# Output projection of a two-layer decoder trunk in fp32r pieces, with its weights split during the attention

## The reference, cut to what matters

```python
def nsa_mixer(h, w_in, w_out, ...):
    q, kc_raw, vc_raw, ks, vs, kw, vw, gates = jnp.split(h @ w_in, splits, axis=-1)
    ...
    o = g[:, :, 0] * heads(o_cmp) + g[:, :, 1] * heads(o_slc) + g[:, :, 2] * heads(o_win)
    return o.reshape(B, S, D_MODEL) @ w_out
def moba_mixer(h, w_in, w_out):
    q, k, v = jnp.split(h @ w_in, 3, axis=-1)
    ...
    return _merge_chunks(o) @ w_out
def reference(x, ...):
    for layer in range(DEPTH):
        mix = nsa_mixer(...) if layer % 2 == 0 else moba_mixer(...)
        x = layer_norm(DN_ALPHA * x + mix, ln_g[layer, 0], ln_b[layer, 0])
        ffn = grouped_moe(x, router_w, router_bias, moe_w_gate[layer], moe_w_up[layer], moe_w_down[layer])
        x = layer_norm(DN_ALPHA * x + ffn, ln_g[layer, 1], ln_b[layer, 1])
    return x
```

## Time and profile before

| what | us |
|---|---|
| median of 3 runs | 779.02 (777.27 to 779.57) |
| profiled execution, its own time | 778.95 |
| span in its profile | 777.2 |
| PE busy in the span | 740.8 (95%) |
| DVE busy | 285.3 (37%) |
| ACT busy | 184.4 (24%) |
| POOL busy | 95.2 (12%) |

### The profile page before, as it was taken

One profiled execution on the slowest core, in us unless ns is written; L12 is line 12 of the kernel. 1 busy time (PEld: TensorE's weight loads), 2 busy tenths in 40 slices (PEclk: granted clock), 3 DMA queues, 4 the chain that ended last, 5 costly groups with the idle time before them and its releaser, 6 DMA issues.

```text
span 777.2 us, 9026 instructions
## 1 busy us (share of the span) xinstructions
PE 740.8 (95%) x3721; PEld 392.2 (50%) x3721; DVE 285.3 (37%) x544; ACT 184.4 (24%) x424; POOL 95.2 (12%) x80
## 2 busy tenths in 40 slices
PE   6999999999999999999969999999999999999984
PEld 5877755556334443443337887645634344434331
DVE  4484676335112211221154774623522121212115
ACT  4443655133011101110131455613300110011100
POOL 0011244212000000000042220411200000000000
PEclk9999999999999999999988999999999999999997
DMA  9999600118899999999999955012799999999991
GB/s 281 367 385 423 280 1 2 55 66 307 341 409 432 428 427 428 428 428 420 421 390 387 387 199 198 20 55 108 280 401 400 429 428 428 429 428 426 421 412 63
DMA packets 41388, 245.05 MB, mean 315 GB/s; under 512 B 5760, under 2 KB 9984, under 8 KB 27008
## 3 DMA queue, kind: packets, MB, share of 16 engines
q1 hardware_dynamic: 41344, 244.43, 78.2%
HBM read 243.37 MB, written 1.05 MB: 315 GB/s over the span
## 4 chain that ended last, share of the span: by engine, by line
PE 80%; DMA 8%; DVE 8%; issue 2%; ACT 1%; SPq 0%; POOL 0%; DVEq 0%
PE ps L751 24%; PE ps L772 13%; DMA ring<-in_w_up 7%; PE ps L674 7%; PE ps L522 4%; PE ps L524 4%; PE ps L523 4%; PE ps L736 3%; PE ps L782 3%; PE ps L615 2%; PE ps L599 1%; PE ps L681 1%; PE ps L539 1%; PE ps L580 1%; PE ps L540 1%
## 5 line engine op out<-in xcount | busy, mean ns | idle before, releaser
L751 PE MATMUL ps<-ring,R 128*64 128x512 f32 x928 | 227.1, 595 | 0.0
L751 PEld LDWEIGHTS ps<-ring,R 128*64 128x64 f32 x928 | 70.5, 137 | 108.5 <-issue 106.9
L772 PE MATMUL ps<-ring,R 128*64 128x512 f32 x448 | 113.5, 596 | 0.0
L1001 ACT ACTIVATE wh<-ps,small 128x512 fp32r<-128x512 f32 x32 | 22.0, 688 | 264.7 <-PE ps L772 263.1
L1284 DVE TENSOR_TENSOR wl<-ring,wh 128x512 fp32r<-128x512 f32 x72 | 54.9, 778 | 46.6 <-ACT wh L979 46.3
L772 PEld LDWEIGHTS ps<-ring,R 128*64 128x64 f32 x448 | 35.2, 137 | 66.9 <-issue 63.8
L1478 DVE SCALAR_TENSOR_TENSOR wl<-ps,small,wh 128x512 fp32r<-128x512 f32 x32 | 24.0, 751 | 104.7 <-ACT wh L1001 104.0
L674 PE MATMUL ps<-ring,R 128*128 128x512 f32 x128 | 57.9, 598 | 0.9 <-DVE R L1591 0.9
L522 PE MATMUL ps<-wh,xh 128*128 128x512 f32 x144 | 57.9, 402 | 0.7 <-DVE wl L1284 0.6
L979 ACT CAST wh<-ring 128x512 fp32r<-128x512 f32 x72 | 44.4, 621 | 55.1 <-PE ps L524 51.5
L523 PE MATMUL ps<-wl,xh 128*128 128x512 f32 x144 | 56.9, 395 | 0.0
(11 more groups left out here) (177 smaller groups left out, 951.4 us busy)
## 6 DMA issues: line engine op xcount, KB each, us to landing
ring<-in_w_gate SPq DMA_DIRECT2D x28, 2048.0 KB, 16.9
ring<-in_w_up SPq DMA_DIRECT2D x22, 2048.0 KB, 18.0
ring<-in_w_down SPq DMA_DIRECT2D x22, 2048.0 KB, 19.6
ring<-in_w_in SPq DMA_DIRECT2D x22, 1024.0 KB, 14.2
ring<-in_w_down SPq DMA_DIRECT2D x12, 1024.0 KB, 26.5
ring<-in_w_out SPq DMA_DIRECT2D x8, 1024.0 KB, 14.7
R<-in_w_up SPq DMA_DIRECT2D x4, 2048.0 KB, 17.7
ring<-in_w_up SPq DMA_DIRECT2D x8, 1024.0 KB, 15.8
```

The costliest lines, as they stand in the source:

```text
L751: last = mm(ps[64 * e:64 * e + 64, to, :], xe[:, j, at + 64 * e:at + 64 * e + 64], slots[e][:, j * UNIT:(j + 1) * UNIT], start=(j == 0), s ...
L772: last = mm(ps[64 * e:64 * e + 64, 2 + w, :], hT[:, k, 64 * e:64 * e + 64], slots[e][:, at:at + UNIT], start=(k == 0), stop=(k == FJ - 1))
```

## The change

**Output projection.** In layer 0 pieces 0 to 6, in layer 1 pieces 0 to 4, of both halves, become three fp32r products each (`PIECED`); the others stay in float32. The high parts of these weights (`WO_HI`) are cast on ACT during the attention, behind the exponentials of an item, by the table `WO_AT` (so many pieces behind item m): one behind each item from 2 to 15 in layer 0 (14 pieces), and 1, 2, 1, 2, 1, 2, 1 behind items 1 to 7 in layer 1 (10 pieces). They go to `xh`, `xl`, `wh`, `wl`, which are free then. The rest of an item's first piece is subtracted on POOL behind the scaling of that item, over the weights in the slot; a second piece's rest is subtracted on DVE, one step later, behind the copy of the probabilities. The attention's own output is split on DVE as it leaves PSUM, a cast and a subtraction in place of one copy. PE waits for all rests of the layer before the first piece.

**Filling products.** `keep_warm` adds products of 128x512 whose result nobody reads: 9 ahead of the first transposes of layer 0 and 7 behind them, 14 and 5 in layer 1. At the start they work on tiles that DVE sets to zero (`blank`). The transposes of tile 1 stand behind piece 6 (layer 0) and piece 4 (layer 1) of tile 0.

**Layer norm behind the experts.** `ln_scale` writes to PSUM, over its own source, and `ln_shift` reads it there. The statistics of tile 1's first half stand behind tile 0's layer norm.

**Order.** SP loads the whole first unit ahead of the second tile of x, and loads the second norm's weights (and waits for the normalised rows) behind all of the layer's experts. ACT starts the first unit's casts one piece into the tokens' casts; it casts the first tile's rows behind `rows_copy(1, 0)` and `score(0)`. ACT and DVE load the count of full slots in the second pair of experts and not behind all of them. Y, the routing's copy of the rows, lies in R4 and no longer in R2.

The diff, cut to its core:

```diff
+        R5r, R6r = R56r[:, 0:3 * D], R56r[:, 3 * D:6 * D]
+        OT_HI = [R6r[:, 1536 + j * S:1536 + (j + 1) * S] for j in range(6)] + [R5r[:, 2560:2560 + S]]
+        OT_LO = [R2r[:, j * S:(j + 1) * S] for j in range(7)]
+        OT2_HI = [R6r[:, 1536 + u * 512:2048 + u * 512] for u in range(3)]
+        OT2_LO = [R2r[:, u * 512:(u + 1) * 512] for u in range(3)]
+        flat = [v[:, :, :].rearrange("p j t -> p (j t)").rearrange("p (n c) -> p n c", c=UNIT) for v in (xh, xl)]
+        WO_HI = [[flat[0][:, 0], flat[0][:, 1], flat[1][:, 0], flat[1][:, 1], wh[:, 0], flat[0][:, 2], flat[0][:, 3]],
+                 [flat[1][:, 2], flat[1][:, 3], wh[:, 1], wh[:, 2], wl[:, 0], wl[:, 1], wl[:, 2]]]
+        PIECED = [7, 5]
+        WO_AT = [[0] * 2 + [1] * 14, [0] + [1, 2] * 3 + [1]]
+        WO = [[(w, j) for w in range(2) for j in range(n)] for n in PIECED]
...
-        Y = R2[:, :].rearrange("p (a c) -> p a c", a=T)
+        Y = R4[:, :].rearrange("p (a c) -> p a c", a=T)
...
+        def wo_lo_at(l, w, j):
+            return slot_r[SLOT_OF[AT[("unit", OUT[2 * l + w])]]][:, j * UNIT:(j + 1) * UNIT]
...
+        def wo_chunks(l, m):
+            first, many = sum(WO_AT[l][:m]), WO_AT[l][m]
+            return [(first + n, WO[l][first + n]) for n in range(many)]
...
-            load_unit(0, 0, 1)
+            load_unit(0)
             sp.dma_start(X[:, 1], x[P:2 * P]).then_inc(x_in[1], 16)
-            load_unit(0, 1, 2)
...
-                sp.wait_ge(N.x_ready, ready(2 * l, T - 1, 1))
-                load_ln(2 * l + 1, R.ln_in)
                 load_halves(6 * PAIRS * l + SLOT + 1)
                 for n in range(SLOT + 3, LASTROUND):
                     load_expert(6 * PAIRS * l + n)
                 for n in range(LASTROUND, 6 * PAIRS, 2):
                     load_halves(6 * PAIRS * l + n)
+                sp.wait_ge(N.x_ready, ready(2 * l, T - 1, 1))
+                load_ln(2 * l + 1, R.ln_in)
...
+            def keep_warm(bank, n):
+                for _ in range(n):
+                    mm(ps[:, bank, :], identb[:, :], bc(causalb[:, :], 1, 4), start=True, stop=True, skip_group_check=True)
...
-                        if a == 0 and j == 3:
+                        if a == 0 and j == (6, 4)[l]:
...
+                if a == 0 and w == 0 and js.start == 0:
+                    pe.wait_ge(wo_lo, (14, 24)[l])
                 for j in js:
                     if a == 0 and w == 0:
                         pe.wait_ge(L.ot_sb, B.ot_sb + j + 1)
-                    if a == 0 and j % 4 == 0:
-                        pe.wait_ge(*landing(("unit", u), j // 4))
-                    last = mm(ps[:, 2 * a + w, :], OT[j][:, a * P:(a + 1) * P],
-                              in_slot(("unit", u))[:, j * UNIT:(j + 1) * UNIT],
-                              start=False, stop=(j == KJ - 1), skip_group_check=True)
+                    if a == 0 and j == PIECED[l]:
+                        pe.wait_ge(*landing(("unit", u), 1))
+                    to, tok = ps[:, 2 * a + w, :], slice(a * P, (a + 1) * P)
+                    if j >= PIECED[l]:
+                        last = mm(to, OT[j][:, tok], in_slot(("unit", u))[:, j * UNIT:(j + 1) * UNIT],
+                                  start=False, stop=(j == KJ - 1), skip_group_check=True)
+                    else:
+                        mm(to, OT_HI[j][:, tok], WO_HI[w][j], start=False, stop=False, skip_group_check=True)
+                        mm(to, OT_HI[j][:, tok], wo_lo_at(l, w, j), start=False, stop=False, skip_group_check=True)
+                        last = mm(to, OT_LO[j][:, tok], WO_HI[w][j], start=False, stop=False, skip_group_check=True)
...
+                keep_warm(4 if l == 0 else 1, (9, 14)[l])
+                if l == 0:
+                    pe.wait_ge(ident_in, 16)
                 transpose_x(l, 0)
+                keep_warm(4, (7, 5)[l])
...
-                    x_hi(0)
-                    first_unit_hi()
+                    x_hi(0, (0,))
+                    first_unit_hi(range(0, 1))
+                    x_hi(0, (1,))
+                    first_unit_hi(range(1, KJ))
...
+                    for n_, (w, j) in wo_chunks(l, m):
+                        act.wait_ge(*landing(("unit", OUT[2 * l + w]), j // 4))
+                        copy(WO_HI[w][j], in_slot(("unit", OUT[2 * l + w]))[:, j * UNIT:(j + 1) * UNIT]).then_inc(wo_hi, 1)
...
                 for i in range(PAIRS):
                     n, g = PAIRS * l + i, DUOS * l + i // 2
+                    if i == 1:
+                        act.wait_ge(R.over, rbase[l].over + 1)
+                        most = act.value_load(over[0:1, 0:1], min_val=0, max_val=S)
                     act.wait_ge(rd.gate_done, n + 1)
...
+                    if a == 0 and w == 0:
+                        act.wait_ge(L.mix, B.mix + 3)
...
+                rows_copy(1, 0)
+                score(0)
                 rows_hi(0, 0)
                 rows_hi(0, 1)
-                rows_copy(1, 0)
-                score(0)
...
+                    for n, (w, j) in wo_chunks(l, m):
+                        if n == wo_chunks(l, m)[0][0]:
+                            pool.wait_ge(wo_hi, len(WO[0]) * l + n + 1)
+                            tt(wo_lo_at(l, w, j), in_slot(("unit", OUT[2 * l + w]))[:, j * UNIT:(j + 1) * UNIT], WO_HI[w][j],
+                               ALU.subtract).then_inc(wo_lo, 1)
...
-                    ln_scale(t, w, bank).then_inc(dve_step, 1)
+                    ln_scale(t, w, bank, ps[:, bank + w, :] if k % 2 else None).then_inc(dve_step, 1)
...
-                    ln_shift(t, w).then_inc(N.x_ready, 1)
+                    ln_shift(t, w, ps[:, bank + w, :] if k % 2 else None).then_inc(N.x_ready, 1)
...
+                    split_x(0, 0, (0,))
...
+                    for c, (w, j) in wo_chunks(l, m - 1)[1:] if 1 <= m < n else []:
+                        dve.wait_ge(wo_hi, len(WO[0]) * l + c + 1)
+                        tt(wo_lo_at(l, w, j), in_slot(("unit", OUT[2 * l + w]))[:, j * UNIT:(j + 1) * UNIT], WO_HI[w][j],
+                           ALU.subtract).then_inc(wo_lo, 1)
                     if m >= 4 and m % T:
                         dve.wait_ge(L.pv, B.pv + m - 3)
                         u = (m - 4) // T
-                        if l == 0:
+                        if l == 0 and u < 7:
+                            step(copy(OT_HI[u], ps[:, 6 + u % 2, 0:S]))
+                            tt(OT_LO[u], ps[:, 6 + u % 2, 0:S], OT_HI[u], ALU.subtract).then_inc(L.ot_sb, 1)
+                        elif l == 0:
                             copy(OT[u], ps[:, 6 + u % 2, 0:S]).then_inc(L.ot_sb, 1)
+                        elif u < 2:
+                            step(copy(OT2_HI[u], ps[:, 6 + u % 2, :]))
+                            tt(OT2_LO[u], ps[:, 6 + u % 2, :], OT2_HI[u], ALU.subtract).then_inc(L.ot_sb, 2)
+                        elif u == 2:
+                            step(copy(OT_HI[4], ps[:, 6 + u % 2, 0:S]))
+                            tt(OT_LO[4], ps[:, 6 + u % 2, 0:S], OT_HI[4], ALU.subtract).then_inc(L.ot_sb, 1)
+                            copy(OT[5], ps[:, 6 + u % 2, S:2 * S]).then_inc(L.ot_sb, 1)
...
-                half_stats(1, 0, 6, main.comb, n + 2)
                 step(half_stats(0, 1, 4, main.comb, n + 3))
                 layer_norm(2 * l + 1, 0, 4, R.ln_in, C.ln_in + 32)
+                half_stats(1, 0, 6, main.comb, n + 2)
```

## The result

The changed kernel takes 773.35 us (median of 13 runs, 770.99 to 776.04) against 777.83 us before (median of 13 runs): the ratio is 0.9936, with a 95% interval of 0.9924 to 0.9948, so 4 to 6 us are won. The forecast was 769.6 us in a range of 764.5 to 775.0. The direction and the range hold; the size does not: about half of the 9.3 us arrived. The kernel before is 1.1 us faster here than the 778.95 us that the forecast started from, so the gap in the time, 3.8 us, looks smaller than the gap in the gain, 4.3 to 4.8 us.

The account below looks back on a forecast made before the run. The prediction took PE as the bound (80% of the span), plus attention's ring and the layer boundary. From 778.95 us, -7.8 + 0.3 + 2.9 - 1.8 - 2.9 = -9.3 gave 769.6 us, range 764.5 to 775.0.

Parts of the forecast that it names:

- The products: Output projections: fp32r pieces gain 0.16 us each, 7.8 us in all, 4.55 in layer 0 and 3.25 in layer 1.
- Rival (e): Output projections: fp32r pieces with both operands newly written are no cheaper; 777.4 us; chance 0.08, shared with Rival (c).
- The row splits moved behind the scores are read only behind the whole projection: Projection and routing: moving these splits was listed under what changes nothing, 0 us.
- Layer 1's splits: Layer 1's attention: three weight splits on DVE delay items 3, 5 and 7; +2.9 us, bounds 0 and 3.3.
- Rival (b): Layer 1's attention: the splits fit; 766.7 us, or 765 if the boundary gives its best; chance 0.13.
- Layer 0's splits: Layer 0's attention: POOL's subtractions fit its gaps, the two-item step stays 6.5 us; +0.3 us, bounds 0 and +3.
- Rival (d): Attention: POOL's queue becomes the ring, splits delay scalings; +26.9 us instead of 3.2, 793 us; chance 0.04.
- Start and boundary: Kernel start and between layers: filling products keep the clock up, first product 0.6 us sooner; gains 1.8 and 2.9 us.
- Rival (a): Start and boundary: filling products do not hold the clock, 1.8 and 2.3 us not won; 773.7 us; chance 0.13.
- The experts: Experts' stage: transfers wait for slots that PE frees, so the stream moves with the stage; no change.
- Rival (c): Experts' end is set by bytes, so the projections' 7.8 us return as PE waits; 777.4; chance 0.08, shared with Rival (e).

Follow-up runs that it names:

- the control: The changed kernel run again with nothing changed, for a second profile (an execution of 772.07 us): median 774.35 us, ratio 0.9948 to the kernel before.
- the first kernel with everything together: Changed kernel with four pieces a half in layer 1, POOL's row rests behind the choice, thirteen filling products at the start: 769.55 us, 0.9871 of before.

## Why the prediction was right, and where its terms were wrong

**The products: right.** A piece is three steps of 0.23 us, as in rows 3; this is the changed kernel in layer 0's projection:

```profile
147.35 0.39 PE L704 MATMUL ps<-slot_r,R_r 128*128 128x512 f32 x1
147.58 0.39 PE L705 MATMUL ps<-xh,R_r 128*128 128x512 f32 x1
147.81 0.40 PE L703 MATMUL ps<-xh,R_r 128*128 128x512 f32 x1
```

Measured were 3.44 us for the forecast's 4.55 and 2.32 for 3.25, because PE waits for the choice. With the wait taken away (POOL's row rests behind the choice) layer 0 gives 46.45 - 42.00 = 4.45 us and layer 1 46.75 - 43.25 = 3.50. Rival (e) is out.

**"The row splits moved behind the scores are read only behind the whole projection": the step that failed.** The edit was priced at nothing because its reader was late. What it issues was not asked for: a POOL instruction that holds SBUF against DVE, at the one place where DVE is on the path. It cost 2.2 us in two layers, the largest miss, and the prediction had no rival for it.

**Layer 1's splits: right mechanism, wrong size.** Forecast +2.9, measured 4.0 with the clock up. A rest took 1.68 us and not 1.42; item 7's share was held to be hidden behind the seeds and was 0.66. Item 3 (0.9 forecast, 1.08 measured) and item 5 (2.85 and 3.29 in all) were near, though the prediction's own terms, 0.9, 1.42 and 0.68, add up to 3.0 and not 2.85. Rival (b), that they fit, is out; its 765 us, too, would by the boundary's bound of 3.9 be 765.7. What the forecast left out is the clock: PE's longer rest ahead of item 5. In the changed kernel's first profile PE rests 2.42 us ahead of item 5's transposes and the clock then falls, so its seeds take 3.14 us instead of the 1.98 of the kernel with layer 1 in float32:

```profile
501.27 1.09 PE L621 MATMUL ps<-cst,R 128*128 128x128 f32 x8 [2.42 <-POOL R L1269]
502.29 1.12 PE L637 MATMUL ps<-R 128*64 128x128 f32 x8
503.34 3.14 PE L710 MATMUL ps<-X,cst 128*128 128x512 f32 x4
```

The Trainium skill's page "SBUF — State Buffer", section "SBUF: two separate sides", says that a VectorE instruction with two SBUF inputs and a GpSimd one that reads SBUF exclude each other for the whole instruction; the forecast's time by it was about 2 us, and it took the row's 1.42. The measured 1.68 lies between them, and the mechanism is the page's: DVE's rests wait for POOL's end. The runs agree with the page at four places: 0.68 against 1.68 us for a rest, 0.18 against 1.50 for a step of 128x16, 0.43 against 1.76 for the one-hot, 1.41 against 3.42 for two shifts whose source is PSUM or SBUF.

**Layer 0's splits: right.** The period of two items is 6.49 us, from the scaling at 116.55 to that at 123.04, and POOL's rests stand in its gaps:

```profile
116.55 1.89 POOL L1269 TENSOR_TENSOR R<-R,small 128x1024 f32<-128x1024 f32 x1 [0.53 <-DVE small L1418]
118.40 1.27 POOL L1273 TENSOR_TENSOR slot_r<-ring,xh 128x512 fp32r<-128x512 f32 x1
...
123.04 1.89 POOL L1269 TENSOR_TENSOR R<-R,small 128x1024 f32<-128x1024 f32 x1 [0.54 <-DVE small L1418]
```

The 0.3 us were 0.0 against the kernel with both projections in float32. Rival (d) is out.

**Start and boundary: right where the clock holds.** The control has -1.71 and -3.52 us for the forecast's -1.8 and -2.9; of the 3.52, 1.03 is the first product's earlier place (0.6 forecast) and 2.49 the faster products behind it (2.3 forecast). The first profile, whose clock fell in both, has -0.14 and -2.13. Rival (a) was put as yes or no for the kernel; the runs show that both happen, from one execution to the next. The profile of 772.07 us has both terms in full, and the median of its six runs is 774.35: some 2 us of the forecast are there in a good execution and not in the median one. The range held because it reached to this case, not because the terms were right. That the 773.35 us lie next to rival (a)'s 773.7 is luck: the choice of experts and layer 1's attention, 3.4 us together, are in the measured time and not in that rival. The forecast should have given the clock two values and not one.

**The experts: right.** Reached 5.4 us sooner in the control, the stage is 0.35 us longer, so the transfers do move with PE. Rival (c) is out; its place, the last pair's halves, is where PE rested 2.16 us instead of 1.32 in one profile of the first kernel with everything together.

**In sum**, in the control's profile, with the clock up at the start and the boundary: -9.3 us forecast, -7.13 measured. The 2.2 us between them are 2.1 for the two projections, where the choice of experts came late (1.16 and 0.95), and 1.3 for layer 1's attention, less 0.7 in layer 0's attention, 0.6 at the boundary and 0.5 in layer 1's experts, and 0.5 more spread over the rest.

## What to carry to other kernels

An edit that only moves an instruction is priced by what that instruction holds while it runs, not only by who reads its result: on POOL and DVE ask what the other engine does in that time, and give a DVE step on the path a PSUM source, or a time at which POOL rests. Splitting operands for cheaper products pays where the splitting engine has idle time ahead of its next step on the path; where it has not, take fewer pieces (here five pieces a half in layer 1 lost 3 us against none, and three were level with none). And where a gain hangs on the clock, one profile is one draw: look at the mean clock of all runs before a term is called won or lost.

## What the runs showed of the hardware

Small DVE steps with two SBUF inputs suffer as much as large ones beside POOL: 128x16 elements took 1.50 us instead of 0.18, as long as POOL's instruction of 512 columns did, and the two engines' instructions then alternated (1.32 and 1.50 us beside POOL's 3.15 for two). The same program had a mean granted clock of 0.983 to 0.996 over its 13 runs. The kernel before, whose PE rested 3.92 us between the layers, stayed at 0.982 to 0.987 in the 48 runs beside the experiments, and the changed kernel without its filling products at 0.977 to 0.987. The clock does not explain all of the spread: the changed kernel has 5.0 us between its fastest and slowest of 13, and the kernel before 4.3 in the 13 beside them.
